# Three attention stages: vector and score work in another order, a smaller ring for the outputs, and one projection moved by one pair of heads

## The reference

```python
# neighbourhood attention (16 heads of 64; latents also see all 256 context tokens)
s = concatenate([q @ k_window + bias, q @ k_ctx]); y = softmax(s) @ [v_window, v_ctx]
y_ctx = softmax(q_ctx @ k_ctx) @ v_ctx
# sliding window (16 query heads, 4 key heads), blocks of 128 queries, 3 blocks of keys
s = concatenate([mask(q @ k_near), q @ k_ctx, sink]); y = softmax(s) @ [v_near, v_ctx]
# differential attention (8 heads, causal)
a = softmax(q1 @ k1) - lam * softmax(q2 @ k2); y = rmsnorm(a @ v) * silu(z)
# then y @ w_out is added to the residual (the first two with a gate)
```

## Time and profile before

| what | value |
|---|---|
| median of three runs | 3423.45 us |
| profiled execution: its time, its span | 3422.99 us, 3421.2 us |
| PE busy | 2927.8 us (86%) |
| DVE, ACT, POOL busy | 1540.5, 1069.2, 754.5 us |
| mean granted TensorE clock | 0.923 of full |
| loop of the first stage (turn of group 0 to the last output projection) | 290.85 to 746.20 us |
| loop of the second stage | 1438.67 to 1691.80 us |
| loop of the third stage with its last projection | 2189.57 to 2502.30 us |

### The profile page before, as it was taken

One profiled execution on the slowest core, in us unless ns is written; L12 is line 12 of the kernel. 1 busy time (PEld: TensorE's weight loads), 2 busy tenths in 40 slices (PEclk: granted clock), 3 DMA queues, 4 the chain that ended last, 5 costly groups with the idle time before them and its releaser, 6 DMA issues. The chain is left out here.

```text
span 3421.2 us, 40822 instructions
## 1 busy us (share of the span) xinstructions
PE 2927.8 (86%) x15820; PEld 2285.7 (67%) x15820; DVE 1540.5 (45%) x2517; ACT 1069.2 (31%) x1800; POOL 754.5 (22%) x168
## 2 busy tenths in 40 slices
PE   7968999977999996998788998699878778499886
PEld 2336777756888885766567776577656666387774
DVE  0133344354334344556544434555555666414444
ACT  0024454543212222465422222433422222332221
POOL 0011111111323231211123333222222222133332
PEclk9979999998999998899989999899988888799997
DMA  7821111011111121111012221211111111122221
GB/s 287 303 101 48 36 47 61 24 48 37 62 61 62 60 74 46 37 38 38 25 62 74 86 86 66 72 62 62 62 44 60 51 49 49 37 99 77 83 74 49
DMA packets 54281, 239.53 MB, mean 70 GB/s; under 512 B 4116, under 2 KB 22036, under 8 KB 29848
## 3 DMA queue, kind: packets, MB, share of 16 engines
q1 hardware_dynamic: 54168, 237.99, 19.5%
HBM read 235.87 MB, written 2.10 MB: 70 GB/s over the span
## 5 line engine op out<-in xcount | busy, mean ns | idle before, releaser
L227 POOL TENSOR_TENSOR w_lo<-w_raw,w_hi 128x2048 fp32r<-128x2048 f32 x117 | 539.2, 4608 | 1465.2 <-ACT w_hi L222 1465.2
L259 PE MATMUL bank<-u_hi,w_hi 128*128 128x512 f32 (+1 forms) x1792 | 683.2, 381 | 53.9 <-DVE u_lo L375 36.0
L260 PE MATMUL bank<-u_lo,w_hi 128*128 128x512 f32 (+1 forms) x1792 | 668.1, 373 | 0.0
L261 PE MATMUL bank<-u_hi,w_lo 128*128 128x512 f32 (+1 forms) x1792 | 666.9, 372 | 0.0
L259 PEld LDWEIGHTS bank<-u_hi,w_hi 128*128 128x128 f32 x1792 | 346.7, 193 | 138.6 <-issue 40.0
L261 PEld LDWEIGHTS bank<-u_hi,w_lo 128*128 128x128 f32 x1792 | 346.5, 193 | 58.6
L260 PEld LDWEIGHTS bank<-u_lo,w_hi 128*128 128x128 f32 x1792 | 347.5, 194 | 54.1 <-issue 1.7
L641 DVE SCALAR_TENSOR_TENSOR resid<-bank,mod,resid 128x512 f32<-128x512 f32 (+1 forms) x384 | 242.3, 659 | 189.8 <-PE bank L261 189.2
L259 PE MATMUL bank<-hid_hi,w_hi 128*128 128x512 f32 (+1 forms) x768 | 278.5, 363 | 39.1 <-POOL w_lo L227 37.6
L222 ACT ACTIVATE w_hi<-w_raw 128x2048 fp32r<-128x2048 f32 x117 | 223.2, 1907 | 190.7 <-PE bank L261 189.5
L260 PE MATMUL bank<-hid_lo,w_hi 128*128 128x512 f32 (+1 forms) x768 | 275.7, 359 | 0.0
(11 more groups left out here) (358 smaller groups left out, 4655.8 us busy)
## 6 DMA issues: line engine op xcount, KB each, us to landing
w_raw<-stream SPq DMA_DIRECT2D x165, 1024.0 KB, 4.8
ada_more<-stream SPq DMA_DIRECT2D x24, 1024.0 KB, 4.8
w_raw<-stream SPq DMA_DIRECT2D x44, 512.0 KB, 4.5
bias<-bias SPq DMA_DIRECT2D x8, 896.0 KB, 4.6
resid<-h SPq DMA_DIRECT2D x1, 3072.0 KB, 17.9
out<-resid SPq DMA_DIRECT2D x1, 2048.0 KB, 7.3
w_raw<-stream SPq DMA_DIRECT2D x4, 256.0 KB, 3.5
cos_sin<-cst SPq DMA_DIRECT2D x1, 512.0 KB, 7.6
```

The costliest lines, as they stand in the source:

```text
L227: pool.tensor_tensor(m.wl[:, s, 0:width], m.raw[:, s, 0:width], m.wh[:, s, 0:width].bitcast(F32), ALU.subtract).then_inc(m.lo_split, 1)
L259: pe.matmul(out, lh, rh, start=start, stop=False)
L260: pe.matmul(out, lh, rl, start=False, stop=False)
L261: return pe.matmul(out, ll, rh, start=False, stop=stop)
```

## The change

- All three stages: `normalise(G+1)` (or `combine(G+1)`) follows `maximum(G+1)` at once on DVE. `gated`, `rotate`, `normalise_qk(j, 0)` and the additions of the third stage, which stood between or before, come behind it; the additions now also come behind `silu`, `output_norm` and `low_y`.
- First stage: the weighed output of latent groups goes to bank 0 of the set. `scores` waits for `set_free` before its first piece, and writes context A (bank 2), B (bank 1), A (bank 0), context B (bank 2). `weigh` of the context group no longer waits itself.
- First stage: the ring of `y_hi` and `y_lo` has three places instead of four, and the third output projection stands beside pair 6 instead of pair 7.

```diff
-        yh, yl = sb("y_hi", [P, 4, TOK], F32R), sb("y_lo", [P, 4, TOK], F32R)
+        yh, yl = sb("y_hi", [P, 3, TOK], F32R), sb("y_lo", [P, 3, TOK], F32R)
...
-        beside = {1: ("vv", 1), 2: ("wo", 0), 3: ("vv", 2), 4: ("wo", 1), 5: ("vv", 3), 7: ("wo", 2)}
+        beside = {1: ("vv", 1), 2: ("wo", 0), 3: ("vv", 2), 4: ("wo", 1), 5: ("vv", 3), 6: ("wo", 2)}
...
-                        ins = act.activation(yh[:, i % 4, t * P:t * P + P], banks(G)[:, 2, 0:P], ACT.Copy)
+                        ins = act.activation(yh[:, i % 3, t * P:t * P + P], banks(G)[:, 0, 0:P], ACT.Copy)
...
                     if G + 1 < len(groups):
                         maximum(G + 1)
+                        normalise(G + 1)
                     kind, x = beside.get(i, ("-", 0))
                     if t >= 2 and kind == "wo":
                         gated(x, (0, 2, 3)[t - 2])
                     if t == 1 and j < PAIRS:
                         normalise_qk(j, 0)
                     low_y(G)
-                    if G + 1 < len(groups):
-                        normalise(G + 1)
...
+                    if G >= 2:
+                        pe.wait_ge(*set_free[G % 2].at(G // 2))
                     if t < NEAR:
-                        pe.matmul(s[:, 0, :], q[A_, c], k[A_, 0:LAT], start=True, stop=True)
-                        pe.matmul(s[:, 1, :], q[B_, c], k[B_, 0:LAT], start=True, stop=True)
-                        if G >= 2:
-                            pe.wait_ge(*set_free[G % 2].at(G // 2))
                         pe.matmul(s[:, 2, 0:CTX], q[A_, c], k[A_, LAT:TOK], start=True,
                                   stop=True).then_inc(first_ctx.sem)
+                        pe.matmul(s[:, 1, :], q[B_, c], k[B_, 0:LAT], start=True, stop=True)
+                        pe.matmul(s[:, 0, :], q[A_, c], k[A_, 0:LAT], start=True, stop=True)
                         pe.wait_ge(*first_ctx.at(NEAR * i + t + 1))
...
# second stage
                         maximum(G + 1)
+                        normalise(G + 1)
...
-                    if G + 1 < len(units):
-                        normalise(G + 1)
...
# third stage
                         maximum(G + 1)
-                        for k in between[0:2]:
-                            add(j - 1, k)
                         combine(G + 1)
-                        for k in between[2:4]:
-                            add(j - 1, k)
...
+                        if j and i + 1 < H and t < 2:
+                            for k in range(4 * t, 4 * t + 4):
+                                add(j - 1, k)
+                        if i + 1 == H:
+                            for k in ((0, 1), (2, 3), (4,), (5,))[t]:
+                                add(j - 1, k)
-                add(H // 2 - 2, 5)
                 add(H // 2 - 2, 6)
```

More of the change, by code:

```diff
@@ L1075, in high_y @@
                     if t < NEAR:
-                        ins = act.activation(yh[:, i % 4, t * P:t * P + P], banks(G)[:, 2, 0:P], ACT.Copy)
+                        ins = act.activation(yh[:, i % 3, t * P:t * P + P], banks(G)[:, 0, 0:P], ACT.Copy)
                     else:
-                        ins = act.activation(yh[:, i % 4, LAT:TOK], banks(G)[:, 2, 0:CTX], ACT.Copy)
+                        ins = act.activation(yh[:, i % 3, LAT:TOK], banks(G)[:, 2, 0:CTX], ACT.Copy)
                     ins.then_inc(y_high.sem)
@@ L1180, in low_y @@
                     dve.wait_ge(*y_high.at(G + 1))
-                    q, o = (slice(t * P, t * P + P), banks(G)[:, 2, 0:P]) if t < NEAR else (
+                    q, o = (slice(t * P, t * P + P), banks(G)[:, 0, 0:P]) if t < NEAR else (
                         slice(LAT, TOK), banks(G)[:, 2, 0:CTX])
-                    dve.tensor_tensor(yl[:, i % 4, q], o, yh[:, i % 4, q].bitcast(F32),
+                    dve.tensor_tensor(yl[:, i % 3, q], o, yh[:, i % 3, q].bitcast(F32),
                                       ALU.subtract).then_inc(set_free[G % 2].sem)
@@ L1290, in output @@
                             for p in range(2):
-                                y = (2 * j + p) % 4
+                                y = (2 * j + p) % 3
                                 c = slice(k * P, k * P + P)
@@ L1343, in weigh @@
                     pe.wait_ge(*copied.at(G + 1))
-                    if t == NEAR and G >= 2:
-                        pe.wait_ge(*set_free[G % 2].at(G // 2))
                     if t == 0 and i % 2 == 0:
@@ L1357, in weigh @@
                                     :, 2, hd * CTX + (b - 4) * P:hd * CTX + (b - 3) * P]
-                                ins = pe.matmul(s[r, 2, 0:P], vp[:, b, r], p, start=(b == 0), stop=(b == 5))
+                                ins = pe.matmul(s[r, 0, 0:P], vp[:, b, r], p, start=(b == 0), stop=(b == 5))
                     ins.then_inc(weighed.sem)
```

## The result

The changed kernel takes 3528.99 us, the median of four executions (3521.01 to 3532.18), against 3423.78 (3422.99 to 3429.84) for the kernel before: ratio 1.030, 95% interval 1.0279 to 1.0321. The forecast was 3494 with a range up to 3525. The direction is right, the size is 35 us short. The profiled execution took 3519.14 (span 3517.3), 96.1 more than the one of before; the four timed ones spanned 3518.6 to 3530.3 us at a mean granted clock of 0.913 to 0.907, the longer the lower. So 96 of the 105 us can be followed in the trace, and the other 9 cannot.

The account below looks back on a forecast made before the run. PE was taken to bound the kernel, with 85 us idle in the three loops to win back. 3423.0 + 21 (first stage) + 10 (second) + 25 (third) + 15 (clock) = 3494 us; 8-in-10 range 3455 to 3525.

Parts of the forecast that it names:

- first: 14 covered scores: First stage, t = 0 and 1 of pairs 0 to 6: new order of scores gains 0.75 us each, -10.4.
- first: beside value projections: First stage, pairs 1, 3 and 5: only the earlier `turn` at t = 2 gains, 0.4 us each, -1.
- first: nine groups beside output projections, at full clock: First stage: PE's third use waits for `gated` behind `normalise(G+1)`, 3 x 9.4 = +28.2 us.
- first: the clock in them: First stage: slower PE clock after the nine waits beside output projections, 0.6 us each.
- first: five groups with nothing beside: Pair 0, t = 2 to 4, and pair 7, t = 0 and 1: `scores` after `normalise` lengthens them, +5.3 us.
- first: the moved projection and the rest of pairs 6 and 7: Third output projection fills three short groups in pair 6, leaves three in pair 7; -1 us.
- second: Second stage: rotation or `gated` behind `normalise` delays `low_y` and the next group; +10 us, bounds 0 and +16.
- third, its clock included: Third stage: late additions delay PE in heads 3, 5 and 7, +25 us, plus 2 us clock for each of five waits.
- clock term: All loops: PE's clock falls after new idle stretches, +15 us, bounds 0 and +35.
- the clock falls behind every new gap: Rival: each of 14 new gaps costs 2.5 us of clock, giving 3514 us or more; chance 0.12.
- Second bank: First stage, beside output projections: PE's third use waits for the bank `gated` frees, 3.4, 2.8 and 3.2 us.
- Scores: First stage: one latent `scores` takes 1.5 us instead of 2.24, a gain of 0.75; bounds 1.4 and 2.24.

Follow-up runs that it names:

- e3: All first-stage edits alone on the kernel before, plus 14 unread matmuls of 512 columns in each output-projection stall; 3464.02 us, ratio 1.0108.
- e11: Kernel before with only the third output projection moved from pair 7 to pair 6 in the first stage; 3426.19 us, ratio 1.0007.
- e1: All first-stage edits alone on the kernel before, stages two and three unchanged; 3477.74 us, ratio 1.0153.
- e13: As e1, plus three unread float32 matmuls between `weigh` and the late `scores` in groups with nothing beside; 3468.03 us, ratio 1.0128.
- e2: As e1, but `gated` stands before `normalise(G+1)` again, as in the kernel before; 3435.76 us, ratio 1.0030.
- e10: Kernel before with second-stage `normalise(G+1)` moved ahead only in groups where DVE has no rotation and no `gated`; 3425.68 us, ratio 1.0006.
- e7: Third-stage edit alone on the kernel before, plus unread matmuls filling the waits of heads 3 and 5; 3454.19 us, ratio 1.0082.
- e12: Kernel before with only the first stage's DVE order changed: `normalise(G+1)` directly behind `maximum(G+1)`; 3468.60 us, ratio 1.0134.
- e15: As e14, plus early `normalise(G+1)` in four groups: three of the first stage, one of the second; 3412.17 us, ratio 0.9958.
- e5: Kernel before with the first stage's new order of scores only where other products stand ahead of `scores`; 3419.63 us, ratio 0.9981.
- e14: As e5, plus three unread float32 matmuls ahead of `turn` in t = 3 of heads 2, 4 and 6; 3412.15 us, ratio 0.9962.

## Why the prediction was right in direction and wrong in size

Turn to turn, profiled executions, in us:

| term | forecast | measured |
|---|---|---|
| first: 14 covered scores | -10.4 | -10.0 |
| first: beside value projections | -1 | -0.7 |
| first: nine groups beside output projections, at full clock | +28.2 | +31.9 (e3) |
| first: the clock in them | +5.4 | +13.4 |
| first: five groups with nothing beside | +5.3 | +12.9 |
| first: the moved projection and the rest of pairs 6 and 7 | -1 | +4.2 (1.9 at full clock in e11) |
| second | +10 | +18.8 |
| third, its clock included | +35 | +29.5 |

**The failed step is the size of the clock term.** The text took 0.6 us for each of nine first-stage waits and none for the second stage or for the groups with nothing beside. Measured in the first stage are 13.4 us in the nine groups (about 1.5 each) and about 8.6 behind the gaps with nothing beside (e1 less e13, with 1.1 of it in the group after them), 22 against 5.4. In the second stage the groups t = 0 of pairs 1, 3, 4, 5 and 7, which follow the lengthened ones, are 8.6 us longer at clocks of 0.68 to 0.85, where nothing was booked. No run filled these, but the windows of pair 1, t = 0, before and after, show what grew:

```profile
1471.33:1481.11 9.78, 9.72 (x58) 6.99 (x57) 5.35 (x14) 6.35 (x13) 0.00 (x0) 1.00 0.01 2
1523.55:1534.91 11.36, 11.30 (x57) 8.19 (x56) 4.72 (x13) 6.34 (x13) 0.00 (x0) 0.85 0.01 1
```

PE is idle for 0.06 us in both, and its busy time for the same work is 1.58 longer. In the third stage the four groups of heads 3 and 5 lose 7.4, near the 8 booked for them. Together that is some 38 us, above the upper bound of 35, against 15 in the sum. Turn to turn the loops lost 100 us where the terms come to 71.5; 23 of the missing 28.5 are the clock, the other 6 are direct costs (62 against 56). The median of the timed executions lies another 10 us above the profiled one, which no trace explains.

The reason given was a misreading. "In the short groups of pair 6, idle for as long, the clock stayed at 1.00" compared the idle time of a whole group. PE's gaps in that group of the kernel before are these:

```profile
684.72 1.53 PE L1358 MATMUL bank<-pt,v 128*64 128x128 f32 x24 [1.54 <-ACT pt L1070]
...
688.97 0.77 PE L1331 MATMUL bank<-cst_sb,e 128*128 128x128 f32 x5 [1.66 <-DVE e L1169]
```

They are two pieces of at most 1.66 us. The new waits are 2.64, 3.12 and 3.73 us in one piece, and in all nine groups of the changed kernel half clock followed. The gap of head 2 is of this kind (3.78 us in one piece ahead of the `turn` of t = 3) and was the row to go by. That the length of the single gap decides is argued from these rows, not shown: in e13 pair 4, t = 3 has the same wait of 2.65 us and stays at full clock:

```profile
588.10:600.47 12.37, 8.93 (x71) 7.27 (x69) 5.03 (x11) 3.55 (x10) 1.19 (x1) 1.00 0.24 87
```

The rival "the clock falls behind every new gap", 3514 or more at a chance of 0.12, comes nearest; the profiled execution took 3519. But its sum is right by luck: the nine gaps of the first stage cost 1.5 each and not 2.5, and 17 of the 38 us lie behind gaps that it does not count.

**Second bank.** Right, in place, number and length: waits of 3.73, 2.64 and 3.12 against 3.4, 2.8 and 3.2. The direct cost was 3.7 us higher than forecast because t = 3 and 4 are some 0.4 and 0.9 us longer even without the wait (9.72 and 9.52 in e2 against 9.34 and 8.62).

**Scores.** 1.49 against 1.5, and 0.75 in each covered group. On the page "TensorE: Matmul & The Clock Gate", Part 3, the Trainium skill says that matmuls start and end in program order, from which the forecast had worked out 1.7. The trace agrees with the order (the four pieces start at 436.24, 436.25, 436.78 and 437.21) and not with the 1.7: the rows of L1307 to L1312 give 1.49, so the hole that the forecast derived from it does not arise. That the order of scores costs elsewhere was booked as +1.2 for a group with nothing beside. It is +1.3 at full clock (8.65 in e2), and 2.2 to 2.9 with the clock. Only one of the five such groups (pair 0, t = 2) has the context group's scores behind it, so the forecast's own prices give 5.6 and not 5.3.

**Second stage.** The chain was right: t = 3 of the even pairs 0, 2 and 4 takes 9.42, 9.50 and 10.46 against 9.2, and e10 shows that the rotation and `gated` behind `normalise` are the whole of it. What came on top is the clock of the groups behind.

**Third stage.** Head 3 at full clock: 16.91 and 17.59 (e7) against 17.0 and 17.4. The clock added 2.7 and 2.0. The stage came out 5 us under its sum because a few groups elsewhere (head 1, t = 1; head 2, t = 3; head 6, t = 3) happened on a better clock than in the profile of before.

## What to carry to other kernels

When a reordering makes the busiest engine wait, price the wait twice: its own length, and what the matmuls behind it take at half clock, and read the second from rows with a gap of that length in one piece, not from the idle sum of a stretch; give it a range, since the same gap does not always bring it. Before an operation goes ahead on an engine that has time to spare, ask which buffer the one it overtakes would free: here DVE's slack of 125 us was real, but the linear banks and the rotation had none. The earlier `normalise` wins 1.2 us in a group where nothing hangs on what it overtakes (10.90 to 9.73, e12 and e15) and loses 3.1 to 9.9 where something does (second stage t = 3 of pair 0, head 3 t = 0). A better order inside one helper can be a loss where it moves a wait ahead of work that used to cover it; apply it only where the wait has long come (e5).

## What the hardware showed that was not expected

- Matmuls that nobody reads made kernels faster: 14 of 512 columns in a wait of 3.73 us took the pieces behind it from 0.21 back to 0.12 us apart, and nine such places gave back 13.7 us (e3). Three float32 ones ahead of three `turn`s bring a kernel from 0.9981 to 0.9962 of before (e14; the intervals just touch, the three windows show it clearly).
- The clock is not a fixed function of a gap. Single gaps of 2.56 us were enough for it in e1, where pair 7, t = 0 and 1 take 10.03 and 10.16 us at 0.85 and 0.84, and 8.79 and 8.80 filled (e13); yet in e2 the first of them has the same gap and takes 8.65 at 1.00. Pair 0, t = 3 and pair 6, t = 3 of e5 have the same gaps (2.06 and 1.54 us); the first took 9.22 us at 0.63, the second 6.77 at 1.00, and in e14 it is the other way round.
- Between executions the kernel before moves by 14 us (3418.75 to 3432.93), yet groups with the same work at clock 1.00 repeat within 0.03 us from kernel to kernel (0.1 beside output projections of the first stage). Edits worth a few us are read more exactly from such windows than from medians.
